# A hybrid attention and state-space block on one core: dense pieces in 26 of 28 attention steps, the second merge gate among them, and GpSimd's low parts at other steps

## The chip, the cores and the metric
The kernel runs on one core of a Trainium2 chip. A time is microseconds of device time of one execution. The kernel before took 439.01, 440.55 and 440.67 us in three runs, median 440.55.

TensorE multiplies (its plain name in the rows is PE, its weight loads PEld), VectorE is DVE, ScalarE is ACT, GpSimd is POOL, and SyncE (SP) issues nearly all DMAs. SBUF is the working memory, PSUM the eight accumulation banks of 128 x 512 float32 that TensorE writes.

## What is computed
One block for 512 tokens of width 1024, in float32:

```python
h = rmsnorm(x, norm_g)
(q, kc, vc, ksl, vsl, kwi, vwi, gl, gate_nsa, u, gate_s5, mg) = split(h @ w_in)
# NSA: 8 heads in 2 groups; three branches, each softmax(q k) v
#   compressed keys (compress(kc), compress(vc)), selected blocks (ksl, vsl, rotary), window (kwi, vwi, rotary)
o_nsa = sum over branches of sigmoid(gl) * branch
branch_a = (o_nsa * silu(gate_nsa)) @ w_proj_nsa
# S5: 32 groups of 16 channels, 64 complex states, diagonal recurrence over the tokens
y = Re(C scan(A, B u)) + D u;  z = gelu(y)
o_s5 = z * sigmoid(z @ w_glu + b_glu)
branch_b = (o_s5 * silu(gate_s5)) @ w_proj_s5
merged = sigmoid(mg_a) * branch_a + sigmoid(mg_b) * branch_b
out = rmsnorm(x + merged @ w_out, final_g)
```

## The kernel before
**Precision by three products.** Each large matmul is done as three of the faster float32r type: both factors are split into a high part and a low part (the rest), and TensorE adds high x low, low x high and high x high (`mm3`, L1043 to L1045). ScalarE makes the high part of each weight block (`split_hi`, L768), GpSimd the low part (L723, `lo_done`), from raw blocks that SyncE loads three ahead in a fixed order (`weight_blocks`). A block's split buffers are two, so its high part waits until the block two ahead of it is used. A dense job is one 128 x 512 output in a bank, over 8 K tiles (4 for the `glu` jobs) of three matmuls each.

**Order by hand.** There is no scheduler: each engine's program is written out, and `bank_plan` numbers the fills and reads of each PSUM bank, so that `open_bank`, `wait_fill` and `wait_drained` are waits on two semaphores for each bank.

**The S5 part.** States are computed in chunks of 4 tokens. Inside a chunk the output needs the products KR (lag by lag) shifted down by 48, 32, 16 and 0 rows within each half of the partitions: the table TT. Before, TensorE does the shift with a matrix of ones (`shift`, a constant that is loaded) and the identity, into banks TT0 and TT1 (L1181), between the jobs kc and vc, and ScalarE copies the two banks out. TT is used first by the Y matmuls (L1289), just ahead of attention. Y goes through memory to be reordered (`y_through_scratch`, 16 stores of L552, then one load of yT). VectorE adds D u to yT (L1850), ScalarE makes the GELU of it (L988), which needs a table load before it and one behind it, and VectorE and GpSimd split z for the GLU.

**Attention.** 24 steps, six for each of four head pairs (two branches, three sets of query tiles: tile 3 alone, tiles 0 and 1, tile 2), and four more turns for what trails. In step s each engine does, in this order:
- TensorE: scores of s (L1320), transposes of the probabilities of w = s - 3 (L1338), a dense piece if `FILL` has one for s, and the weighted values of w - 1 (L1359). Where a new job starts right behind another piece, the values go ahead of the piece. The values of a head pair add up in bank 6; the first of a pair (L1351, from peT) waits until VectorE has taken the last pair out.
- VectorE: the copy of the transposed probabilities of w out of bank 4 (L1813; for some w that of bank 5 too, else ScalarE does it), in steps 10, 16 and 22 `gate_pair` (L1788, and L1790 the high part), the product of a dense job that ended in step s - 1 (`fill_part`, L1778, and for a glu job L1770, L1470 and L1776), the masking with its row minimum (L1804), and `normalise` of s - 1 (L1827).
- ScalarE: copies of bank 5, the exponentials of s (L975), and the tanh of a job that ended in s (L942).
- GpSimd: low parts, each held back by `behind_normalise(s)` until VectorE has normalised step s, which is at the end of VectorE's step s + 1.

`FILL` names the first and last step of each dense job. All go to bank 7 but those in `FILL_BANK`. `D_TERM_AT`, `GELU_AT` and `Z_SPLIT_AT` say in which steps the sum with D, the GELU and the high part of z are done. Behind the loop, the merge gates MA and MB and the projections A and B follow for eight column blocks (the B jobs need all of f, the A jobs the low part of the last head pair), then the output projection, the residual and the last norm, whose four row tiles are stored in halves (L643, L645).

Before, gn1 runs in steps 0 to 5, gn2 in 6 to 9, glu0 in 12 and 13, glu1 in 15 and 16, gn3 in 18 to 20, glu2 in 22 and 23, glu3 in 24 and 25 (bank 0), MB0 in 26 and 27 (bank 1), and MB1 behind the loop.

Of the kernel before, what the change touches and what calls it, by code (L numbers as in the profile page):

```python
# [19 lines left out]
F32 = mybir.dt.float32  # L20
# [5 lines left out]
P = 128  # L26
# [47 lines left out]
O_LOW_AHEAD = ["gn3", "glu1"]  # L74
F_LOW_AFTER = ["gn3", "glu1", "mgb0", "mgb1"]
O_LOW_AFTER = ["mgb0", "pb0"]


# [20 lines left out]
def tile_offsets(tiles):  # L99
# [22 lines left out]
D_TERM_AT, GELU_AT, Z_SPLIT_AT = (4, 5), (6,), (7, 8)  # L122
BOTH_COPIES = (3, 4, 5)
# [3 lines left out]
LOW_BEHIND = dict(gn3=10, glu1=16, mgb0=20)  # L127
O_LOW_BEHIND = (9, 15, 21)
F_LOW_BEHIND = (13, 17, 23)


def bank_plan():
# [42 lines left out]
    use("TT0", 0)  # L175
    use("TT1", 1)
# [49 lines left out]
def build_program(nc, a, out):  # L226
# [16 lines left out]
    with ctx:  # L243
# [3 lines left out]
        def shared(name, size, *sets):  # L247

            made = {}
            for tensors in sets:  # L250
                with ExitStack() as once:
# [50 lines left out]
                   [("TT", [P, GP, CH, SC], F32), ("below_u", [P, 1024], F32), ("U_sh", [P, GP, NCH], F32)],  # L302
# [3 lines left out]
        TT, U_sh, yT, f_hi, f_lo = (m[n] for n in ("TT", "U_sh", "yT", "f_hi", "f_lo"))  # L306
# [5 lines left out]
        m = shared("room_5", 640, [("KR", [P, GP, SC], F32), ("shift", [P, CH - 1, P], F32)],  # L312
                   [("hidn", [GROUPS * NC, 2, 256], F32)], [("k_hi_0", [P, T], F32R)])
        KR, shift, hidn, k_hi_0 = (m[n] for n in ("KR", "shift", "hidn", "k_hi_0"))
# [91 lines left out]
        khi_done, qhi_done, k_split, q_split = (sem(n) for n in ("k_hi_done", "q_hi_done", "k_split", "q_split"))  # L406
        starts_set, pool_carry = sem("run_starts_set"), sem("gpsimd_carry")
# [116 lines left out]
        def _(sp):  # L524
# [41 lines left out]

            def load(dst, src, s):
                sp.dma_start(dst, src).then_inc(s, 16)
# [27 lines left out]
            for k, (name, split) in enumerate(blocks):  # L596
# [4 lines left out]
                if k == NRAW + 2:  # L601
                    const_loads()
# [47 lines left out]
        def _(pl):  # L650
            pl.wait_ge(dt_row_in, 16)
            nc.gpsimd.tensor_copy(par_rows[0:GP, 2, :].rearrange("p (r n) -> p r n", r=2),
                                  dt_in[0:GP, :].unsqueeze(2).broadcast_to((GP, 2, SN))).then_inc(dt_spread, 1)
            nc.gpsimd.memset(flat_k[:, :, :, NC - 1:NC], 0.0).then_inc(flat_zero, 1)
            nc.gpsimd.memset(kcT[:, :, :], 0.0).then_inc(kc_zero, 1)
            nc.gpsimd.memset(flat_v[:, :, :, NC - 1:NC], 0.0).then_inc(flat_zero, 1)
# [17 lines left out]
            def query_low(n, s=None):  # L674

                pl.wait_ge(qhi_done, n + 1)
                if s is not None:
                    behind_normalise(s)
                nc.gpsimd.tensor_tensor(qr_lo[:, n, :], qr[:, n, :], q_hi[n].bitcast(F32),
                                        ALU.subtract).then_inc(q_split, 1)  # L680

# [20 lines left out]
            for j, name in enumerate(split_names):  # L702
# [6 lines left out]
                if name == "gn3":  # L709
                    query_low(2, 8)  # L710
                if name in O_LOW_AHEAD:
                    c = O_LOW_AHEAD.index(name)
                    pl.wait_ge(ohi_done, c + 1)
                    behind_normalise(O_LOW_BEHIND[c])
                    nc.gpsimd.tensor_tensor(oT_lo[:, c, :], tmp[:, 1, :], oT_hi[:, c, :].bitcast(F32),
                                            ALU.subtract).then_inc(oT_split, 1)
# [1249 lines left out]
```

## Time and profile before
| what | value |
|---|---|
| timed runs | 439.01, 440.55, 440.67 us |
| the profiled execution | 440.01 us, its span 438.2 us |
| TensorE busy | 420.4 us, 96% |
| VectorE / ScalarE / GpSimd busy | 281.6 / 200.9 / 169.4 us |
| mean granted clock of TensorE | 0.988 of full speed |
| attention, first scores to the end of MB1 | 152.63 to 266.96 us |

A row of the timeline has start, duration, engine, line, operation, output <- inputs and how often, and in brackets how long the engine was idle before it and for whom. The granted clock is 1.00 at 2.4 GHz and 0.50 at 1.2 GHz.

### The profile page before, as it was taken

What the parts mean: (1) busy time and instruction counts of PE and PEld (TensorE: products, weight loads), DVE (VectorE), ACT (ScalarE), POOL (GpSimd) and SP (SyncE); (2) the same over time, 40 slices, a digit from 0 to 9 for tenths busy, and PEclk for the clock granted to TensorE, in tenths of its full rate; (3) what the DMA queues carried; (4) which work ended last, traced back from release to release, by engine and by line L of the source; (5) the groups of instructions that cost most, each with busy time, mean ns of one, the idle gap of its engine ahead of it and who ended that gap; (6) DMA issues with size and microseconds to landing.
All of it is one profiled execution on the core that took longest, in us unless ns stands there. A gap on an engine that the chain in (4) does not pass through costs nothing.

```text
span 438.2 us, 7325 instructions
## 1 busy us (share of the span) xinstructions
PE 420.4 (96%) x2776; PEld 342.4 (78%) x2776; DVE 281.6 (64%) x641; ACT 200.9 (46%) x394; POOL 169.4 (39%) x92
## 2 busy tenths in 40 slices
PE   5899999999999997899999999999999999999994
PEld 5788888898778875667677778888888888888994
DVE  3779996999999997699998952071071071170544
ACT  6644759714235675857467432222222222231433
POOL 0444323333369402154141344454454454454430
PEclk9999999999999999799999999999999999999998
DMA  8998993224841254101001113933333333333105
GB/s 286 153 276 209 177 250 111 60 71 120 249 96 49 51 99 144 48 2 49 1 6 46 49 49 101 328 79 113 100 81 111 97 88 101 101 96 97 48 1 191
DMA packets 71458, 48.05 MB, mean 110 GB/s; under 512 B 20272, under 2 KB 66816, under 8 KB 71424
## 3 DMA queue, kind: packets, MB, share of 16 engines
q1 hardware_dynamic: 71264, 47.53, 41.8%
q8 instruction: 22, 0.36, 0.4%
q14 instruction: 12, 0.10, 0.1%
q10 hardware_dynamic: 160, 0.07, 0.1%
HBM read 43.39 MB, written 4.19 MB: 109 GB/s over the span
## 4 chain that ended last, share of the span: by engine, by line
PE 86%; DVE 5%; DMA 3%; issue 2%; SPq 2%; ACT 1%; POOL 1%; POOLq 1%; DVEq 0%; ACTq 0%
PE bank L1043 23%; PE bank L1045 22%; PE bank L1044 22%; PE bank L1359 3%; PE bank L1338 3%; PE bank L1320 2%; PE bank L1211 2%; SPq L552 2%; DMA yT<-y_scratch 1%; DVE prob L1804 1%; PE bank L1088 1%; DVE prob L1827 1%; PE bank L1157 1%; DMA hid<-in_norm_g 1%; DVE probT L1813 1%
## 5 line engine op out<-in xcount | busy, mean ns | idle before, releaser
L723 POOL TENSOR_TENSOR w_lo<-raw,w_hi 128x1024 fp32r<-128x1024 f32 (+3 forms) x56 | 133.8, 2388 | 181.2 <-ACT w_hi L768 166.8
L1043 PE MATMUL bank<-hT_lo,w_hi 128*128 128x512 f32 x288 | 115.7, 402 | 4.6 <-DVE tmp L1778 3.4
L1045 PE MATMUL bank<-hT_hi,w_hi 128*128 128x512 f32 x288 | 112.8, 392 | 0.0
L1044 PE MATMUL bank<-hT_hi,w_lo 128*128 128x512 f32 x288 | 112.7, 391 | 0.0
L768 ACT ACTIVATE w_hi<-raw 128x1024 fp32r<-128x1024 f32 (+2 forms) x56 | 58.4, 1043 | 73.9 <-PE bank L1045 73.3
L1043 PEld LDWEIGHTS bank<-hT_lo,w_hi 128*128 128x128 f32 x288 | 54.3, 189 | 18.0 <-issue 7.2
L1045 PEld LDWEIGHTS bank<-hT_hi,w_hi 128*128 128x128 f32 x288 | 54.3, 189 | 11.6
L1044 PEld LDWEIGHTS bank<-hT_hi,w_lo 128*128 128x128 f32 x288 | 54.4, 189 | 10.5
L975 ACT ACTIVATE prob<-prob,nmax 128x128 f32<-128x128 f32 (+2 forms) x64 | 35.3, 553 | 27.1 <-DVE nmax L1804 27.1
L1004 ACT ACTIVATE tmp<-bank 128x512 f32<-128x512 f32 x16 | 9.5, 597 | 59.6 <-PE bank L1045 57.2
L1869 DVE SCALAR_TENSOR_TENSOR tmp<-tmp,bank 128x512 f32<-128x512 f32 x8 | 5.5, 688 | 44.6 <-ACT tmp L1004 44.6
L1864 DVE SCALAR_TENSOR_TENSOR tmp<-tmp,bank 128x512 f32<-128x512 f32 x8 | 5.5, 687 | 40.1 <-ACT tmp L1004 32.7
L1804 DVE CUSTOM_DVE_ANT_0 prob<-bank,causal 128x128 f32<-128x128 f32 (+2 forms) x64 | 27.9, 483 | 0.0
L1827 DVE TENSOR_SCALAR prob<-prob,coef,gate 128x128 f32<-128x128 f32 (+2 forms) x64 | 26.1, 460 | 0.9
L1043 PE MATMUL bank<-w_lo,m_hi 128*128 128x256 f32 (+1 forms) x80 | 26.1, 326 | 0.3 <-POOL f_lo L723 0.3
L1044 PE MATMUL bank<-w_hi,m_lo 128*128 128x256 f32 (+1 forms) x80 | 26.0, 325 | 0.0
L1045 PE MATMUL bank<-w_hi,m_hi 128*128 128x256 f32 (+1 forms) x80 | 26.0, 325 | 0.0
L1338 PE MATMUL bank<-ident,prob 128*128 128x128 f32 x160 | 23.1, 284 | 0.3 <-DVE probT L1813 0.3
L1359 PEld LDWEIGHTS bank<-probT,v_tok 128*64 128x64 f32 x288 | 16.1, 136 | 9.3 <-issue 7.4
L1464 DVE TENSOR_TENSOR bank<-X,bank 128x512 f32<-128x512 f32 (+4 forms) x42 | 22.2, 528 | 1.5
L1359 PE MATMUL bank<-probT,v_tok 128*64 128x128 f32 (+1 forms) x288 | 22.5, 291 | 0.0
L1338 PEld LDWEIGHTS bank<-ident,prob 128*128 128x128 f32 x160 | 17.6, 143 | 6.1 <-issue 4.1
(255 smaller groups left out, 768.5 us busy)
## 6 DMA issues: line engine op xcount, KB each, us to landing
raw<-in_w_in SPq DMA_DIRECT2D x28, 512.0 KB, 3.8
raw<-in_w_in SPq DMA_DIRECT2D x16, 256.0 KB, 4.0
raw<-in_w_out SPq DMA_DIRECT2D x8, 512.0 KB, 3.7
x_sb<-in_x SPq DMA_DIRECT2D x4, 512.0 KB, 5.1
raw<-in_w_proj_s SPq DMA_DIRECT2D x4, 512.0 KB, 3.4
raw<-in_w_proj_nsa SPq DMA_DIRECT2D x8, 256.0 KB, 3.9
r_sb<-in_x SPq DMA_DIRECT2D x1, 2048.0 KB, 8.5
out<-r_sb SPq DMA_DIRECT2D x8, 256.0 KB, 2.2
```

The source lines that it names most:

```text
L723: nc.gpsimd.tensor_tensor(lo, whole, hi.bitcast(F32), ALU.subtract).then_inc(lo_done, 1)
L768: nc.scalar.activation(split_views(name)[0], view(raw, k % NRAW, dims), ACT.Copy)\
L975: nc.scalar.activation(pi, pi, ACT.Exp, scale=-1.0, bias=nmax[:, s % 4, g, k:k + 1], accum_out=den[:, s % 4, g, k:k + 1]).then_inc(e_done, 1)
L1004: drain(nc.scalar.activation(tmp[:, 0, :], bk(f"{kind}{d}")[:, :], ACT.Tanh, scale=0.5), f"{kind}{d}")
L1043: nc.tensor.matmul(dst, w[0], x[1], start=first, stop=False, skip_group_check=True)
L1044: nc.tensor.matmul(dst, w[1], x[0], start=False, stop=False, skip_group_check=True)
L1045: return nc.tensor.matmul(dst, w[0], x[0], start=False, stop=last, skip_group_check=True)
L1338: ins = nc.tensor.transpose(bk(job)[:, col:col + P], prob[:, w % 4, g, c + P * kt:c + P * kt + P], ident[:, :])
L1359: ins = nc.tensor.matmul(o[DH * g:DH * g + DH, P * at[0][0]:P * at[0][0] + n], v_tok[:, kt, b, DH * g:DH * g + DH], probT[:, 2 * (w % 2) + ...
L1464: link(V.tensor_tensor(o, x, y, op))
L1804: drain(V.tensor_tensor_reduce(prob[:, s % 4, g, c:c + n], bk(job)[:, c:c + n], causal[:, T - n:T], 1.0, 3.0e38, ADD, ALU.min, nmax[:, s % ...
L1827: V.tensor_scalar(pi, pi, coef[:, s % 4, g, k:k + 1], gate[:, i, HPG * g + r, 1 + b:2 + b], MUL, MUL)\
```

## The change
The table TT is no longer made on TensorE. GpSimd zeroes a buffer `lags` (behind the low part of u2), SyncE copies KR into it with seven DMAs at the four row offsets (`shifted_lags`, behind the load of kwi), and ScalarE copies `lags` into TT. The constant `shift` is gone, `rope` has a semaphore of its own, and the other four constant loads come later, ahead of kc's load. GpSimd's first small jobs go behind its first low part. The last row tile's first half is stored from ScalarE's queue.

In attention the dense jobs go to other steps: all but 5 and 10 have a piece, MB1 moves into the loop, and only MB1 has another bank than 7. The D term, the GELU and the z split come one step later, as do the steps in which VectorE copies both banks. `gate_pair` goes ahead of the copy and its high part behind it, and GpSimd's low parts of the weights, of oT and of f stand at other steps.

```diff
-FILL = dict(gn1=(0, 5), gn2=(6, 9), glu0=(12, 13), glu1=(15, 16), gn3=(18, 20), glu2=(22, 23), glu3=(24, 25),
-            MB0=(26, 27))
-FILL_BANK = dict(glu3=0, MB0=1)
+FILL = dict(gn1=(0, 4), gn2=(6, 9), glu0=(11, 12), glu1=(13, 14), gn3=(15, 17), glu2=(18, 19), glu3=(20, 21),
+            MB0=(22, 24), MB1=(25, 27))
+FILL_BANK = dict(MB1=1)
...
-D_TERM_AT, GELU_AT, Z_SPLIT_AT = (4, 5), (6,), (7, 8)
-BOTH_COPIES = (3, 4, 5)
+D_TERM_AT, GELU_AT, Z_SPLIT_AT = (5, 6), (7,), (8, 9)
+BOTH_COPIES = (4, 5, 6)
...
-LOW_BEHIND = dict(gn3=10, glu1=16, mgb0=20)
-O_LOW_BEHIND = (9, 15, 21)
-F_LOW_BEHIND = (13, 17, 23)
+LOW_BEHIND = dict(gn3=11, glu1=14, mgb0=18, mgb1=21)
...
+            def shifted_lags():
+
+                wait_drained(sp, "KR")
+                sp.wait_ge(lags_zero, 1)
+                for j in range(CH):
+                    down = SC * (CH - 1 - j)
+                    for first, last in ((0, SN), (SN, P)) if down else ((0, P),):
+                        sp.dma_start(lags[first + down:last, j], KR[first:last - down]).then_inc(lags_in, 16)
...
             def const_loads():
-                load(shift[:, :, :], a["shift"], consts_in)
-                load(rope[:, :, :], a["rope"], consts_in)
...
                 if k == NRAW + 2:
+                    load(rope[:, :, :], a["rope"], rope_in)
+                if k == NRAW + 7:
                     const_loads()
...
+                if name == "kwi":
+                    shifted_lags()
...
             for i in range(NT):
-                sp.wait_ge(y_ready[i], 1)
-                sp.dma_start(out[0, P * i:P * i + P, 0:512], r_sb[:, i, 0:512]).then_inc(stored, 16)
+                if i < NT - 1:
+                    sp.wait_ge(y_ready[i], 1)
+                    sp.dma_start(out[0, P * i:P * i + P, 0:512], r_sb[:, i, 0:512]).then_inc(stored, 16)
...
+                elif name == "gn3":
+                    oT_low(0, 10)
+                    query_low(3, 12)
+                    f_low(0, 13)
+                elif name == "glu1":
+                    f_low(1, 15)
+                    oT_low(1, 16)
+                elif name == "mgb0":
+                    f_low(2, 20)
+                elif name == "mgb1":
+                    f_low(3, 22)
+                    oT_low(2, 22)
+                elif name == "pb0":
+                    oT_low(3)
...
-            pe.wait_ge(consts_in, 16 * 4)
-
-            wait_drained(pe, "KR")
-            for k in range(2):
-                open_bank(pe, f"TT{k}")
...
+                pair_ends = s >= 10 and s % 6 == 4
+                if pair_ends:
+                    gate_pair((s - 10) // 6)
                 if 0 <= w < NS:
                     copy_probs(w)
-                if s >= 10 and s % 6 == 4:
-                    gate_pair((s - 10) // 6)
+                if pair_ends:
+                    pair_high((s - 10) // 6)
```

The order of instructions at two places. The first is VectorE at the start of step 10, with the last rows of step 9. Before:

```order
L1823 RECIPROCAL coef<-den 128x2 [waits exp_done]
L1827 TENSOR_SCALAR prob<-prob,coef,gate 128x384 [waits dve_chain]
L1827 TENSOR_SCALAR prob<-prob,coef,gate 128x384
L1813 COPY probT<-bank4 128x384 [waits pv_done,bank4_filled]
L1788 TENSOR_TENSOR tmp<-bank6,tmp 128x512 [waits bank4_drained,pv_done]
L1790 CAST oT_hi<-tmp 128x512 [waits bank6_drained]
L1778 SCALAR_TENSOR_TENSOR sg_third<-tmp,bank7 128x512 [waits tanh_done]
```

And after:

```order
L1834 RECIPROCAL coef<-den 128x2 [waits exp_done]
L1838 TENSOR_SCALAR prob<-prob,coef,gate 128x384 [waits dve_chain]
L1838 TENSOR_SCALAR prob<-prob,coef,gate 128x384
L1870 CAST z_hi<-z 128x512 [waits z_done] x2
L1796 TENSOR_TENSOR tmp<-bank6,tmp 128x512 [waits bank4_drained,pv_done]
L1824 COPY probT<-bank4 128x384 [waits pv_done,bank4_filled]
L1801 CAST oT_hi<-tmp 128x512 [waits bank6_drained]
L1786 SCALAR_TENSOR_TENSOR sg_third<-tmp,bank7 128x512 [waits tanh_done]
```

The gate of the pair (tmp<-bank6) has moved ahead of the copy, and the second pair of z_hi casts now stands between the normalise of step 8 and the gate.

The second place is GpSimd from the low part of the third query on (qr_lo is a query's, oT_lo a head pair's, f_lo the GLU output's, w_lo a weight block's: gn3, glu1, mgb0 in this order). Before:

```order
L679 TENSOR_TENSOR qr_lo<-qr,q_hi_mid 128x512
L715 TENSOR_TENSOR oT_lo<-tmp,oT_hi 128x512
L723 TENSOR_TENSOR w_lo<-raw,w_hi 128x1024
L679 TENSOR_TENSOR qr_lo<-qr,q_hi_ends 128x512
L665 TENSOR_TENSOR f_lo<-z,f_hi 128x512
L715 TENSOR_TENSOR oT_lo<-tmp,oT_hi 128x512
L723 TENSOR_TENSOR w_lo<-raw,w_hi 128x1024
L665 TENSOR_TENSOR f_lo<-z,f_hi 128x512
L723 TENSOR_TENSOR w_lo<-raw,w_hi 128x1024
```

And after:

```order
L686 TENSOR_TENSOR qr_lo<-qr,q_hi_mid 128x512
L737 TENSOR_TENSOR w_lo<-raw,w_hi 128x1024
L694 TENSOR_TENSOR oT_lo<-tmp,oT_hi 128x512
L686 TENSOR_TENSOR qr_lo<-qr,q_hi_ends 128x512
L672 TENSOR_TENSOR f_lo<-z,f_hi 128x512
L737 TENSOR_TENSOR w_lo<-raw,w_hi 128x1024
L672 TENSOR_TENSOR f_lo<-z,f_hi 128x512
L694 TENSOR_TENSOR oT_lo<-tmp,oT_hi 128x512
L737 TENSOR_TENSOR w_lo<-raw,w_hi 128x1024
```

The weight parts have moved ahead of the low parts of the first and second head pair.

## Rows read from the trace of the kernel before
**Rows 1.** Page, section 2: TensorE's granted clock in 40 slices of 10.95 us.
```profile
PEclk9999999999999999799999999999999999999998
```
**Rows 2.** Waits of TensorE: who waited for whom, us in total, times, longest.
```profile
PE bank L1043 <- DVE tmp L1778: 3.4, 1, 3.4
PE bank L1351 <- DVE tmp L1788: 1.5, 3, 0.9
```
**Rows 3.** Timeline of TensorE around the shift of KR: start us, us, what.
```profile
85.44 0.39 PE L1043 MATMUL bank<-hT_lo,w_hi 128*128 128x512 f32 x1
...
86.13 1.46 PE L1181 MATMUL bank<-KR,shift 128*128 128x256 f32 x6
...
88.55 0.39 PE L1043 MATMUL bank<-hT_lo,w_hi 128*128 128x512 f32 x1
```
**Rows 4.** Timeline of TensorE, steps 5 to 10.
```profile
167.15 0.88 PE L1338 MATMUL bank<-ident,prob 128*128 128x128 f32 x6
...
176.38 0.77 PE L1043 MATMUL bank<-hT_lo,w_hi 128*128 128x512 f32 x1 [3.44 <-DVE tmp L1778]
...
193.22 0.88 PE L1338 MATMUL bank<-ident,prob 128*128 128x128 f32 x6
195.01 1.08 PE L1351 MATMUL bank<-peT,v_blk 128*64 128x512 f32 x4 [0.92 <-DVE tmp L1788]
```
**Rows 5.** Windows: length, busy us of each engine, granted clock, DMA share, GB/s.
```profile
174.50:175.00 0.50, 0.00 (x0) 0.00 (x0) 0.50 (x2) 0.00 (x0) 0.50 (x1) 0.97 0.00 0
...
181.50:182.00 0.50, 0.50 (x5) 0.50 (x5) 0.27 (x1) 0.50 (x2) 0.00 (x0) 0.70 0.00 0
```
**Rows 6.** Timeline of VectorE, step 4: the sum of y with D.
```profile
168.91 1.41 DVE L1850 SCALAR_TENSOR_TENSOR yT<-u_perm,pcol,yT 128x512 f32<-128x512 f32 x2 [2.19 <-DMA yT<-y_scratch]
```
**Rows 7.** Windows of steps 5, 6 and 7 to 9 of VectorE, the third engine.
```profile
170.24:178.40 8.16, 4.71 (x31) 3.54 (x32) 8.09 (x23) 4.25 (x10) 2.54 (x1) 0.79 0.07 11
181.73:193.15 11.42, 11.42 (x95) 8.41 (x93) 11.15 (x36) 8.92 (x22) 5.08 (x4) 1.00 0.01 1
```
**Rows 8.** Timeline of ScalarE around the GELU of z.
```profile
178.42 1.28 ACT L988 ACT_TABLE_LOAD   x1
...
179.72 3.90 ACT L988 ACTIVATE z<-yT 128x512 f32<-128x512 f32 x4
183.63 1.28 ACT L975 ACT_TABLE_LOAD   x1
```
**Rows 9.** Timeline of step 13 on three engines.
```profile
204.22 0.87 PE L1338 MATMUL bank<-ident,prob 128*128 128x128 f32 x6
...
206.40 1.09 PE L1359 MATMUL bank<-probT,v_tok 128*64 128x128 f32 x16
...
204.88 0.54 DVE L1813 COPY probT<-bank 128x384 f32<-128x384 f32 x1
205.34 0.28 DVE L1804 CUSTOM_DVE_ANT_0 prob<-bank,causal 128x128 f32<-128x128 f32 x1
...
207.28 0.49 ACT L975 ACTIVATE prob<-prob,nmax 128x256 f32<-128x256 f32 x1
```
**Rows 10.** Timeline of GpSimd and VectorE: products of z with and without a low part.
```profile
254.22 2.38 POOL L723 TENSOR_TENSOR w_lo<-raw,w_hi 128x1024 fp32r<-128x1024 f32 x1 [1.46 <-ACT w_hi L768]
...
254.49 2.67 DVE L1770 SCALAR_TENSOR_TENSOR z<-tmp,z 128x512 f32<-128x512 f32 x1
...
209.20 0.68 DVE L1770 SCALAR_TENSOR_TENSOR z<-tmp,z 128x512 f32<-128x512 f32 x1
```
**Rows 11.** Timeline of SyncE (loads of kwi and kc) and ScalarE (KR, kc).
```profile
52.13 3.70 SPq L628 DMA_DIRECT2D raw<-in_w_in  x2
...
61.97 0.41 ACT L778 ACTIVATE KR<-bank 128x256 f32<-128x256 f32 x1
...
74.38 1.04 ACT L768 ACTIVATE w_hi<-raw 128x1024 fp32r<-128x1024 f32 x1
```
**Rows 12.** Timeline of SyncE's queue: the last two stores.
```profile
435.11 0.33 SPq L643 DMA_DIRECT2D out<-r_sb  x1
435.49 0.43 SPq L645 DMA_DIRECT2D out<-r_sb  x1
```

More of the change, by code:

```diff
@@ L680, in query_low, with oT_low, f_low @@
                                         ALU.subtract).then_inc(q_split, 1)
+            def oT_low(c, s=None):
+                pl.wait_ge(ohi_done, c + 1)
+                if s is not None:
+                    behind_normalise(s)
+                nc.gpsimd.tensor_tensor(oT_lo[:, c, :], tmp[:, 1, :], oT_hi[:, c, :].bitcast(F32),
+                                        ALU.subtract).then_inc(oT_split, 1)
+            def f_low(t, s):
+                behind_normalise(s)
+                low_part(f_lo, z, f_hi, (t,), fhi_done, f_split)
             def carry_last_groups():
@@ L879, in _ @@
             after("kc")
+            ac.wait_ge(lags_in, 16 * (2 * CH - 1))
             for k in range(2):
-                evacuate(f"TT{k}", TT[:, :, 2 * k:2 * k + 2, :].rearrange("p g j c -> p j g c"),
-                         bk(f"TT{k}")[:, :].rearrange("p (j g c) -> p j g c", j=2, c=SC))
+                lag = slice(2 * k, 2 * k + 2)
+                nc.scalar.activation(TT[:, :, lag, :].rearrange("p g j c -> p j g c"), lags[:, lag], ACT.Copy).then_inc(tt_built, 1)
             after("vc")
@@ L990, in _ @@
                                              ACT.Gelu_apprx_tanh).then_inc(z_done, 1)
-                if s in pieces and s == FILL[pieces[s][0]][1] and pieces[s][0] != "MB0":
+                if s in pieces and s == FILL[pieces[s][0]][1] and pieces[s][0] not in ("MB0", "MB1"):
                     fill_part(pieces[s][0])
+                if s == FILL["MB0"][1]:
+                    after("mgb0")
             for dp in range(4):
@@ L1000, in _ @@
                         wait_fill(ac, f"{kind}{d}")
-                        if gate_first:
-                            after(f"mgb{d}")
+                        if gate_first and d == 1:
+                            after("mgb1")
                         tanh_free(f"{user}{d}")
@@ L1172, in _ @@
             channel_major("kc", "kc")
-            pe.wait_ge(consts_in, 16 * 4)
-            wait_drained(pe, "KR")
-            for k in range(2):
-                open_bank(pe, f"TT{k}")
-                for jj in range(2):
-                    j = 2 * k + jj
-                    down = shift[:, j, :] if j < CH - 1 else ident[:, :]
-                    ins = nc.tensor.matmul(bk(f"TT{k}")[:, 256 * jj:256 * jj + 256], down,
-                                           KR[:, :, :].rearrange("p g c -> p (g c)"), start=True, stop=True,
-                                           skip_group_check=True)
-                fill(ins, f"TT{k}")
             channel_major("vc", "vc")
@@ L1724, in _ @@
             wait_fill(ve, "H")
+            ve.wait_ge(consts_in, 16 * 2)
             for m in range(2):
@@ L1831, in _ @@
                 w = s - LAG
+                pair_ends = s >= 10 and s % 6 == 4
+                if pair_ends:
+                    gate_pair((s - 10) // 6)
                 if 0 <= w < NS:
                     copy_probs(w)
[L1834 to L1836 removed]
+                if pair_ends:
+                    pair_high((s - 10) // 6)
+                if s - 1 in pieces and s - 1 == FILL[pieces[s - 1][0]][1] and pieces[s - 1][0] not in ("MB0", "MB1"):
                     fill_part(fills, pieces[s - 1][0])
```

75 lines of the change are left out of this document (27 added, 48 removed).

## Prediction
> **What bounds the kernel now.** I read three views in this order. The busy slices of the page: TensorE's clock row stands at 9 in nearly every slice, with one 7 at 175 to 186 us [rows 1]. The waits of TensorE: the longest inside the kernel is 3.4 us, for the product that takes gn1's gate out of bank 7 (L1778); three waits of 1.5 us together are for the gate of a finished head pair (L1788) [rows 2]. The timelines around the long wait: TensorE had nothing from 172.94 to 176.38 [rows 4], the granted clock left full speed at 174.98 and came back at about 181.7 [rows 5], so 5.3 us of resumed work ran at 1.2 instead of 2.4 GHz, which lost 2.65 us. So the kernel is bound by TensorE's stream of matmuls; a change gains what it takes from that stream, from its waits, and from the clock that a wait costs. In attention VectorE is close behind: between 170.24 and 193.15 it is idle for no more than 0.35 but in the 3.3 us between 178.40 and 181.73, in which TensorE crawled [rows 7]. A time below is in microseconds of the span of before; the profiled execution took 440.01 (span 438.2 and 1.8 around it), the three timed runs 439.01, 440.55 and 440.67.
>
> **Part 1, the lag table TT by DMA.** TensorE drops 8 matmul records that ran from 86.13 on. vc's second K tile started at 88.55; without them it starts one tile of 0.68 (three matmuls) behind 86.13, at 86.81: 1.74 gained [rows 3]. VectorE's chain up to attention is not fed by it, but its last link, the products of the compressed branch, waits for ScalarE and GpSimd work that does move; I take it as moving along, with 0 to 0.75 lost if one of its products falls under a GpSimd low part. On SyncE seven DMAs for the lags and four constant loads now stand between kwi's load (52.13, [rows 11]) and kc's, and the first waits until KR is out at 62.38 [rows 11]. Eleven issues at 0.33 to 0.43 [rows 12] put kc's load at about 67, landing some 4 later, 3 before ScalarE wants it at 74.38 [rows 11]. That cover hides all of it; vc's load goes with it and is wanted only 7.6 later. The zeroing of the lags and the later small GpSimd work sit in waits. The ScalarE copies stay two.
>
> **Part 2, steps 0 to 10.** The Y round trip through memory made VectorE wait 2.19 at step 4 [rows 6]. Now its sum with D stands in steps 5 and 6, behind more work, and y, which moves 1.74 with TensorE, is there first. That ends the old stall: gn1 is done at step 4, its product is in step 5, and gn2 starts at step 6. What is late next? I walk it. TensorE's transposes of step 5 began at 167.15 [rows 4]; they come 1.74 earlier for part 1 and 1.36 later, since all 8 K tiles of gn1 instead of 6 are ahead of them: 166.8. VectorE's copy follows the start of transposes by 0.66 [rows 9]: 167.4. Its steps 5 to 9 took 19.4 in before (8.16 and 11.42 less a short wait, [rows 7]); now all four sums with D lie in them instead of two (1.33 more, half of [rows 6] being 0.7 each), less 0.1 to 0.4 of blocked time: 20.6. And ScalarE delays it. Its GELU, now behind the exponentials of step 7, takes 1.28 + 3.90 + 1.28 with its table loads [rows 8]. The masking of step 7 starts at 177.5, its exponentials end 2.43 later [rows 9], the GELU and loads end at 186.4, the two exponentials of step 8 at 187.7; VectorE wants them at 186.4 and loses 1.3. Its step 10 begins at 189.3, and the head-pair gate, now first in it, is done at 190.0. TensorE is at that point long before: its transposes of step 10 began at 193.22, 26.07 behind those of step 5 [rows 4]; without stall, slow clock and two K tiles this is 18.6, so 185.4, done at 186.1. So it waits 3.9, at a step that has no dense piece: **the stall moves from step 6 to step 10 and does not shrink**. The values of pair 1 start at 190.0 instead of 195.01: 5.0 ahead. But 3.9 of idling is longer than the 3.44 after which the clock had fallen, so I charge the same 2.65 behind it. The unknown here is 0 to 3.9 for the wait (at 0 if VectorE ran 4 us faster), and 0 or 2.65 for the clock.
>
> On the table loads the Trainium skill ("ScalarE: Activation LUTs", section "What ACT_TABLE_LOAD costs") says that a switch costs a drain of some 1.38 us beside the 1.28 of the load. The trace shows none: the GELU ends at 183.62, the load starts at 183.63 and [rows 8] leave no room for a drain. By that rule the gate would come 2.8 later and the time would be 442.8; the sum goes by the rows.
>
> **Part 3, steps 11 to 27.** Work is the same: 40 K tiles before the first B block on either side. Gone are the other two gate waits, 0.6 [rows 2], since gate_pair now stands ahead of the copy. New is that glu1, gn3, glu2, glu3 and MB0 each start in bank 7 one step after the piece ahead of them ended there, so each waits for a VectorE product. At step 13 TensorE is ready 1.65 behind the start of transposes (0.63 of transposes and 1.02 of values, [rows 9] with the step's end at 207.42); VectorE needs 0.66 + 0.47 + 0.69 [rows 9, 10], so 0.2. But GpSimd's weight parts, 2.38 long, now start with steps 13 and 20, just ahead of the products of glu0 and glu2, and a product with both inputs in SBUF stands until GpSimd ends: 254.49 took 2.67 and ended 0.56 behind the end of the low part, against 0.68 alone [rows 10]. From the walk: step 13 loses 0.7, step 15 1.2 (VectorE is late by then, with f_low under its product), 18 0.25, 20 0.95, 22 0.2: 3.3, of which the range is 1.0 (no collision, five times 0.2) to 5. The skill ("SBUF — State Buffer", "Who interferes with whom") calls this an exclusive lock that goes to the one that issued first; by it and by the rows the loss is the same.
> MB1 inside the loop fills slots but adds no time. Behind the loop the last pair's low part has only B0 and B1 (5.5) to hide under, and needs 2.7, then pa0's low part 2.4: 0.4 is left, so nothing is charged; if one is late, A0 waits 0.5.
>
> **Part 4, the end.** The last two stores now leave from two queues: the second no longer stands behind 0.33 of issue and its gap, 435.49 to 435.11 [rows 12]: 0.35 gained.
>
> **Sum.** 5.0 gained up to pair 1, 2.65 given to the clock, 0.6 gained, 3.3 given to bank 7, 0.35 gained: 0.0. So 440.0 against the profiled execution; the median of the runs is 0.5 above that, and I say 440.3.
>
> **The rivals.** (a) The clock holds, or the wait of step 10 is short enough for it: 2.65 less, 437.6. For it speaks that the clock fell only 2 us into the old idle time, so a wait under 2 would be harmless; against it that my walk has 3.9. (b) VectorE keeps up: wait of step 10 under 1, collisions mild. Then 3.9, 2.65 and about 1.5 of the 3.3 come back: 432.3. For it: its steps hold gaps I may have over-counted; against: they are counted from rows. (c) Slower: the late VectorE of steps 13 to 15 meets f_low(0) and the glu1 part so that gn3's wait in step 15 reaches 3.5 instead of 1.2; from there the clock falls again. 2.3 + 2.65 on top: 445.2. It decides once that wait passes about 2 us. (d) The kc load comes too late, for more bytes are ahead of it: it would have to be over 5 late (3 of cover and 2.7 between GpSimd's part and TensorE's need), and each further one counts in full: 442 or more.
>
> **How the numbers follow.** Forecast 0.58 (own range 438.2 to 442.4, from 1.0 to 5 for bank 7 and 0.75 for the compressed branch), (a) 0.18, (b) 0.10, (c) 0.10, (d) 0.04. The range is 435.5 to 443.5: below it lies most of (b), 0.08, above it some 0.10 of (c) and (d), and it takes in (a) with the bank-7 term at its low end. A measurement here tells 0.5% (2.2 us) from no change. Faster by more, under 438.3: (b), most of (a) and an edge of the forecast, 0.30; slower by more: (c), (d) and an edge, 0.16; within: 0.54.
>
> **What would show it.** The waits of TensorE in the new profile: none at step 6, one of 3 to 4.5 on the peT matmul of pair 1, with a low clock behind it; 0.5 to 1.5 each at the starts of glu1, gn3 and glu3, put down to L1770's product. ScalarE's GELU at 181 to 185 and VectorE idle about 1 us ahead of the normalise of step 8. No row for shift, 1.7 earlier gs0. If TensorE has no wait over 2 us at step 10, the walk of part 2 is wrong, and (a) or (b) holds.

## The result, and the profile after

The changed kernel took **443.18 us** in the median of 6 runs (442.72 to 444.06) against 439.78 for the kernel before (6 runs, 438.66 to 441.11). The ratio on record is 1.0062, 95% interval 1.0039 to 1.0084; the two medians by themselves stand 0.8% apart. It is slower by 0.6%, small but outside its interval, where I had forecast no change (440.3, range 435.5 to 443.5). Its profiled execution took 442.79, with a span of 441.0 against 438.2.

The clock row of the page (section 2, 40 slices, now of 11.0 us) answers to [rows 1]; the waits of TensorE answer to [rows 2] (us in total, times, longest):

```profile
PEclk9999999999999999989999999999999999999999
```

```profile
PE bank L1360 <- DVE tmp L1796: 4.1, 1, 4.1
PE bank L1065 <- DVE z L1778: 2.7, 3, 1.0
PE bank L1065 <- DVE CT L1601: 1.8, 1, 1.8
...
PE bank L1298 <- ACT Y_sb L796: 1.1, 1, 1.1
```

The 3.4 at gn1's gate is gone, and 4.1 on the peT matmul of pair 1 has come, as forecast. So have the starts of glu1, gn3 and glu3 in bank 7 (2.7). But two waits stand there that I had not foreseen: one for CT, one for Y_sb. TensorE's timeline has them all (start us, us, what, wait in brackets); the rows from 187.96 on answer to [rows 4]:

```profile
41.40 0.47 PE L1065 MATMUL bank<-hT_lo,w_hi 128*128 128x512 f32 x1 [1.76 <-DVE CT L1601]
...
150.85 0.45 PE L1298 MATMUL bank<-U_sh,TT 64*64 64x128 f32 x8 [1.07 <-ACT Y_sb L796]
...
187.96 0.88 PE L1347 MATMUL bank<-ident,prob 128*128 128x128 f32 x6
192.97 1.36 PE L1360 MATMUL bank<-peT,v_blk 128*64 128x512 f32 x4 [4.14 <-DVE tmp L1796]
...
207.80 0.47 PE L1065 MATMUL bank<-z_lo,w_hi 128*128 128x512 f32 x1 [0.72 <-DVE z L1778]
...
216.88 0.47 PE L1065 MATMUL bank<-hT_lo,w_hi 128*128 128x512 f32 x1 [1.02 <-DVE z L1778]
...
231.52 0.47 PE L1065 MATMUL bank<-z_lo,w_hi 128*128 128x512 f32 x1 [0.23 <-DVE tmp L1786]
...
240.53 0.47 PE L1065 MATMUL bank<-z_lo,w_hi 128*128 128x512 f32 x1 [0.94 <-DVE z L1778]
```

**The wait at 41.40.** q0 opens the bank that VectorE still reads as CT. VectorE's setup is a chain of some 40 tiny instructions. Here it is in the changed kernel, on VectorE and then on GpSimd (pieces of the two timelines):

```profile
26.27 0.85 DVE L1474 TENSOR_SCALAR s5p<-s5p 128x16 f32<-128x16 f32 x1
...
29.56 2.36 DVE L1471 TENSOR_TENSOR s5p<-s5p,pcol 128x16 f32<-128x16 f32 x1
...
35.09 2.27 DVE L1567 COPY powers<-s5p 128x16 f32<-128x16 f32 x1
...
39.79 0.68 DVE L1598 TENSOR_SCALAR CS<-bank 64x512 f32<-64x512 f32 x1
```

```profile
26.14 0.96 POOL L766 MEMSET lags<- 128x1024 f32 x1
29.50 2.39 POOL L737 TENSOR_TENSOR w_lo<-raw,w_hi 128x1024 fp32r<-128x1024 f32 x1 [2.40 <-ACT w_hi L786]
34.94 2.40 POOL L737 TENSOR_TENSOR w_lo<-raw,w_hi 128x1024 fp32r<-128x1024 f32 x1 [3.05 <-ACT w_hi L786]
```

The zeroing of the lags holds one tiny instruction (0.85 instead of 0.17). By those 0.7 us the chain slides under the low part of u3 (a product of 0.2 takes 2.36) and, 2.7 late by then (35.09 instead of 32.42), under that of q0 (a copy of 0.17 takes 2.27). In the kernel before, the same chain's last product pair began at 29.49 and was through; the low part began at 29.71, and CS was written at 35.00:

```profile
29.49 0.38 DVE L1464 TENSOR_TENSOR s5p<-s5p 128x16 f32<-128x16 f32 x2
...
35.00 0.68 DVE L1591 TENSOR_SCALAR CS<-bank 64x512 f32<-64x512 f32 x1
```

So VectorE comes to CS 4.8 late and TensorE waits 1.76. The Trainium skill ("SBUF — State Buffer", "Who interferes with whom") says that with both inputs in SBUF a product contends with a GpSimd instruction that reads SBUF, and that a copy or a tensor_scalar can contend too; all three kinds stand in these rows, and the trace agrees.

**The wait at 150.85.** ScalarE empties the Y banks behind the exponentials of the compressed branch, and these came late:

```profile
144.69 1.50 DVE L1745 TENSOR_TENSOR e_cmp<-e_cmp,nmax_c 128x512 f32<-128x512 f32 x1
...
146.29 1.28 ACT L941 ACT_TABLE_LOAD   x1 [3.14 <-DVE e_cmp L1745]
...
150.06 1.20 ACT L796 ACTIVATE Y_sb<-bank 128x256 f32<-128x256 f32 x4
```

**Milestones.** The first scores (attention's start) came at 153.63 instead of 152.63; the values of pair 1 at 192.97 instead of 195.01; the first matmul of B0 at 269.71 instead of 267.10; the last matmul at 434.76 instead of 432.00. From the first scores to pair 1 the change gained 3.0, and I had forecast 3.3. The forecast was lost ahead of attention: 1.0 late where I had 1.74 early, which is 2.74 of the 2.8 by which the profiled execution missed it. Behind pair 1 it went a little better than forecast: 4.8 lost up to the last matmul, where I had 5.35.

### The profile page after: what moved, and what is told of

Its sections match the earlier page's. It is cut to its first block, busy times and chain, and to the rows that moved or that the text cites. A ratio compares the mean times of both kernels' runs of the same rounds, so it can differ in the third digit from the quotient of the medians.

```text
span 441.0 us, 7320 instructions
## 1 busy us (share of the span) xinstructions
PE 418.3 (95%) x2768; PEld 338.8 (77%) x2768; DVE 283.1 (64%) x641; ACT 201.2 (46%) x394; POOL 170.8 (39%) x93
## 4 chain that ended last, share of the span: by engine, by line
PE 62%; DVE 23%; ACT 5%; issue 3%; SPq 3%; DMA 2%; POOL 1%; POOLq 1%; DVEq 0%; ACTq 0%
PE bank L1065 17%; PE bank L1067 16%; PE bank L1066 16%; DVE bank L1471 5%; DVE X L1471 5%; PE bank L1329 3%; PE bank L1347 3%; PE bank L1368 3%; DMA raw<-in_w_in 2%; DVE s5p L1471 1%; DVE prob L1815 1%; PE bank L1360 1%; DVE z L1778 1%; ACT w_hi L786 1%; ACT z L1006 1%
## 5 line engine op out<-in xcount | busy, mean ns | idle before, releaser
L1824 DVE COPY probT<-bank 128x384 f32<-128x384 f32 (+1 forms) x24 | 14.4, 599 | 14.1 <-PE bank L1347 14.0
L1368 PE MATMUL bank<-probT,v_tok 128*64 128x128 f32 (+1 forms) x288 | 23.4, 300 | 0.0
```

Source lines behind the costliest of these rows:

```text
L1368: ins = nc.tensor.matmul(o[DH * g:DH * g + DH, P * at[0][0]:P * at[0][0] + n], v_tok[:, kt, b, DH * g:DH * g + DH], probT[:, 2 * (w % 2) + ...
L1824: drain(V.tensor_copy(probT[:, 2 * (w % 2), 0:n], bk(f"PT0_{w}")[:, 0:n]), f"PT0_{w}")
```

## Experiments: where the start is lost

Ten more kernels and a second profile each of the two kernels follow. They ran in three batches, each with its own runs of the kernel before, whose median was 440.17 (e1 to e4), 440.24 (e5 to e8) and 441.05 (e9 to e12); so kernels of different batches are compared by their ratios. In the tables "scores" is the start of the first scores, "to B0" the time from there to the first matmul of B0, "waits" the sum of TensorE's waits in that stretch, and "clock" what it lost by a low clock: busy time times (1 - granted clock), over windows of half a us from 170 to 202.

**e1_zero_later: the zeroing at another place.**

```diff
-                if name == "u2":
+                if name == "q1":
                     nc.gpsimd.memset(lags[:, :, :, :], 0.0).then_inc(lags_zero, 1)
```

> The changed kernel with one instruction moved: GpSimd zeroes the lags behind the low part of q1 instead of behind that of u2. My theory (A): in the profile of the changed kernel the zeroing ran at 26.14 for 0.96 us and held one of VectorE's many tiny instructions (0.85 instead of 0.17); by that 0.7 us the chain behind it slid under two GpSimd low parts (a 0.2 us product took 2.36, a 0.17 us copy 2.27), came 4.8 us late, made TensorE wait 1.76 at the start of q0 (41.40) and, through a late e_cmp, ScalarE drain a Y bank late (1.07 at 150.85). Behind q1 VectorE works out of PSUM, so both waits go: 2.8 less than the changed kernel, about 440.3, and TensorE reaches the first scores at 150.8 instead of 153.6. Rival (B): the two waits come from something else in part 1 (the GpSimd work that now stands behind its first low part, or the order of the loads); then nothing changes, 443.2.

Measured: 442.53 (12 runs), ratio 1.0046, interval 1.0021 to 1.0070. Both theories miss: the wait for CT only shrank to 1.11, and the one for Y_sb stayed (1.05). The timeline says why. Without any zeroing in its way the chain was still caught by the low parts of u3 and q0:

```profile
29.44 2.53 DVE L1471 TENSOR_TENSOR s5p<-s5p 128x16 f32<-128x16 f32 x2
...
34.93 2.51 DVE L1471 TENSOR_TENSOR pwt<-powers 128x32 f32<-128x32 f32 x2
...
40.80 0.47 PE L1065 MATMUL bank<-hT_lo,w_hi 128*128 128x512 f32 x1 [1.11 <-DVE CT L1601]
```

So of the 1.76 in the changed kernel the zeroing itself makes 0.65; the other 1.11 is a slide that comes without it.

**e2_zero_in_before: the zeroing added to the kernel before.**

```diff
+                if name == "u2":
+                    nc.gpsimd.memset(below_u[:, :], 0.0)
```

> The kernel before with one instruction added: GpSimd zeroes 128x1024 elements that nothing reads, behind the low part of u2, where the changed kernel zeroes its lags. Theory (A), the knife edge of the small VectorE chain: the same slide as in the changed kernel, TensorE waits about 1.8 at q0 and up to 1.1 at Y: 1.8 to 2.8 slower than before, 441.6 to 442.6. Theory (B), the zeroing sits in a wait and costs nothing: as before, 439.8.

Measured: 441.11, ratio 1.0015, interval 0.9992 to 1.0039. The wait at q0 is made as in the changed kernel (the tiny instruction takes 0.86, CS comes at 39.91, TensorE waits 1.76), and the first scores are 2.1 late; there is no wait for Y_sb. The time shows only 0.9 of it, and its interval reaches zero. It is also the first sign that the runs of before have part of this loss in them already.

**e3_lags_alone: part 1 without the rest** (the zeroing behind q1's low part; attention and the end as before).

```diff
-                    ins = nc.tensor.matmul(bk(f"TT{k}")[:, 256 * jj:256 * jj + 256], down,
-                                           KR[:, :, :].rearrange("p g c -> p (g c)"), start=True, stop=True,
...
+                    for first, last in ((0, SN), (SN, P)) if down else ((0, P),):
+                        sp.dma_start(lags[first + down:last, j], KR[first:last - down]).then_inc(lags_in, 16)
```

> The kernel before with part 1 alone (TT from shifted copies of KR by DMA, its loads in their new places), the zeroing behind q1's low part, attention and the end as before. By my sum: 1.74 us of TensorE work gone, the loads hidden, so 438.1 (ratio 0.996); the step-6 stall stays, since the Y round trip moves along with TensorE. Rival: the loads that stand 16 us later than before (kc at 71.0 instead of 55.4) or a product of the compressed branch under a low part take some of it back: 438.5 to 439.8.

Measured: 439.56, ratio 0.9986, interval 0.9958 to 1.0014. A slide again (CS at 39.34, 1.12 at q0), and the wait for Y_sb is there too (1.06): it belongs to part 1, not to the slide.

**e4_attention_alone: the changed kernel without part 1**, so TT comes from the shift matmuls and nothing is zeroed.

> The changed kernel without part 1: TT comes from the shift matmuls again, nothing is zeroed, attention, the low parts and the end as changed. The traces give 285.57 us from the first scores to the end in the kernel before and 287.37 in the changed one, so attention and the end cost 1.8 by themselves: 441.6 (ratio 1.004). By my prediction's walk they cost 1.7. Rival: the late VectorE of the first part of the changed kernel is what made its attention slow (step 10's wait of 4.14), and with an early start this is 1 to 3 faster than that: 438.6 to 440.6.

Measured: 443.60, ratio 1.0066, interval 1.0039 to 1.0093, where a ratio of 1.004 was expected, which is just inside the interval. It also slid (CS at 39.35, 1.12 at q0), and it had no wait for Y_sb. The stretch to B0 took 116.77, a little more than in the changed kernel. Since the slide made its first scores late as well (153.96), it says nothing on the rival of an early start; e6_after_gated below does.

So three kernels (e1_zero_later, e3_lags_alone, e4_attention_alone) slid though GpSimd had nothing new ahead of u3's low part but small things of 0.3 us, or nothing at all (e3_lags_alone). The question became whether the kernel before slides as well. Two experiments answer it.

**e11_before_again: the kernel before, a second profile.**

> The kernel before, unchanged, for a second profile. Theory (C): it stands on the edge, so another execution may well show VectorE's tiny product under u3's low part (2.2 us instead of 0.2), VectorE at CS at 39 instead of 35.0 and a wait of TensorE for CT of about 1.1 at q0. Theory (D): it never slides; CS at 35.0 and no such wait.

It took 439.97 (one run) and it slid:

```profile
29.48 2.52 DVE L1464 TENSOR_TENSOR s5p<-s5p 128x16 f32<-128x16 f32 x2
...
40.83 0.47 PE L1043 MATMUL bank<-hT_lo,w_hi 128*128 128x512 f32 x1 [1.10 <-DVE CT L1594]
```

with the low part at 29.58. Of two profiles of the kernel before one slides and one doesn't; the second product of the pair starts some 0.2 behind its first, so at 29.70 against a low part at 29.71 in the one, at 29.69 against 29.58 in the other. In the three kernels above, too, the low part was first (29.55 against 29.65, 29.70 against 29.77, 29.70 against 29.84). **The profile on which I predicted was the lucky one at this place.** Over the whole kernel it was not: it took 440.01 and the one that slid 439.97. The slide brought the first scores 1.15 later, and by pair 1 all of it was made up (195.01 and 194.95), for the wait of step 6 was 0.35 shorter and the low clock happened to cost 1.0 less.

**e5_before_gated, e6_after_gated, e7_lags_gated: the slide made impossible.** GpSimd waits with two low parts until VectorE has left the chains that they could hold. Both low parts still end ahead of TensorE's need. In e6_after_gated and e7_lags_gated the zeroing also stands behind q1's low part.

```diff
+                if name == "u3":
+                    wait_copied(pl, "B")
+                if name == "q0":
+                    wait_copied(pl, "CT0")
```

> The kernel before with two waits added on GpSimd: the low part of u3 starts only when VectorE has begun to read the B bank (its first chain of tiny products is behind it), the low part of q0 only when it has read CT0 (its powers are done). The first batch showed that the slide of VectorE's setup under these two low parts (2.2 + 2.3 us) happens without any zeroing too, in a run of the changed kernel without part 1 and in two with the zeroing later; the shown profile of the kernel before escaped it by some 0.02 us (a product at 29.70, the low part at 29.71). Theory (C), the kernel before stands on that edge by itself and its runs are a mix of both cases: with the waits it never slides, no wait of TensorE at q0, VectorE reads CT0 at 35.0, and the median is 0.5 to 1.5 below that of before. Theory (D), the kernel before never slides and only changed programs do: same as before, or slower by what the low parts lose.

> The changed kernel with the zeroing behind q1's low part and the same two waits on GpSimd. Theory: the wait at q0 (1.76) and the one at Y (1.07) both go, TensorE reaches the first scores at 150.9 instead of 153.6, attention costs what it did (+2 against the kernel before), so 440.3 +- 0.5. Rival: attention is paced by VectorE from step 5 on whatever comes before, and the 2.8 come back as a longer wait at step 10: 442 to 443.

> The kernel before with part 1 alone and the two waits on GpSimd. Theory: no wait at q0 or Y, so part 1 is worth what I said of it, 1.74 us of TensorE against the gated kernel before; 437.5 to 438.3. Rival: the wait of step 6 for gn1's gate, which Y's round trip paces, grows by what the start gains: 439 or more.

| kernel | median | ratio (95%) | CS at | at q0 | for Y_sb | scores |
|---|---|---|---|---|---|---|
| before, first profile | 439.78 | | 35.00 | 0 | 0 | 152.63 |
| before, e11_before_again | 439.97 | | 39.22 | 1.10 | 0 | 153.78 |
| changed | 443.18 | 1.0062 (1.0039-1.0084) | 39.79 | 1.76 | 1.07 | 153.63 |
| e5_before_gated | 439.64 | 0.9993 (0.9975-1.0012) | 35.74 | 0 | 0 | 152.78 |
| e7_lags_gated | 438.43 | 0.9957 (0.9941-0.9974) | 35.72 | 0 | 1.05 | 152.07 |
| e6_after_gated | 441.43 | 1.0024 (1.0013-1.0035) | 35.51 | 0 | 1.05 | 151.77 |

The two waits on GpSimd end the slide in all three; what is left of it is one copy that takes 0.49 instead of 0.17. What follows:
- The slide costs the changed kernel some 0.38% or 1.7 us (1.0062 to 1.0024; by the two intervals 0.1% to 0.6%; first scores 153.63 to 151.77). The kernel before gains 0.07% by them, within its interval; I had expected 0.5 to 1.5 us. That its runs are a mix is shown by its two profiles; how often each case comes, and so why the waits win it so little, is not.
- The wait for Y_sb stays in all with part 1. In the gated kernels the exponentials of the compressed branch start at 143.37 without part 1 and at 144.42 in e6_after_gated; TensorE comes to the Y banks 1.75 earlier (first of them at 145.39 in e7_lags_gated, at 147.14 in e5_before_gated). VectorE's product there takes 1.50 with part 1 (142.82, under a low part that now starts earlier, at 141.37 instead of 143.43) and 0.69 without (142.38). So 0.8 of the 1.05 by which the exponentials come later is this collision; without it, by these rows, a wait of some 0.2 would be left (an estimate, not run).
- So part 1 brings the first scores 0.7 forward, from 152.78 to 152.07, and not 1.74. In time it is worth 1.2 us (439.64 to 438.43): **part 1 alone, gated, beats the kernel before** by 0.43% (0.26% to 0.59%).
- e6_after_gated was to be at 440.3 and is at 441.43; against e7_lags_gated attention and the end cost 3.0. It starts attention earliest of all with the new one, and its stretch to B0 is 116.86: an early start doesn't help.

## Experiments: attention

Eleven profiles have the old attention or the new one under different starts. The stretch to B0, taken apart:

| kernel | attention | to B0 | waits | clock | rest |
|---|---|---|---|---|---|
| before | old | 114.47 | 5.26 | 2.71 | 106.50 |
| e11_before_again | old | 113.25 | 5.11 | 1.71 | 106.43 |
| e3_lags_alone | old | 112.85 | 6.26 | 0 | 106.59 |
| e5_before_gated | old | 113.18 | 5.01 | 1.65 | 106.52 |
| e2_zero_in_before | old | 114.65 | 6.51 | 1.69 | 106.45 |
| e7_lags_gated | old | 114.88 | 5.49 | 3.05 | 106.34 |
| changed | new | 116.08 | 7.05 | 1.71 | 107.32 |
| e12_after_again | new | 116.00 | 7.02 | 1.57 | 107.41 |
| e4_attention_alone | new | 116.77 | 7.04 | 2.54 | 107.19 |
| e6_after_gated | new | 116.86 | 7.04 | 2.64 | 107.18 |
| e1_zero_later | new | 116.75 | 7.05 | 2.43 | 107.27 |

In the mean the new attention takes 2.6 more (116.5 against 113.9): 1.4 of it in waits, 0.4 by the clock, 0.8 in the rest.

**e12_after_again: the changed kernel, a second profile.**

> The changed kernel, unchanged, for a second profile. The slide is to be there in any execution (the zeroing alone shifts the chain by 0.7, far more than its spread of 0.1): a wait of 1.76 for CT at q0, one of about 1.05 for Y_sb, 4.1 at step 10. Open is the low clock behind step 10: 3.35 us of it in the first profile, 1.7 us lost; the profiles of the gated and the later-zeroing kernels show more.

It took 442.98 (one run), with 1.76 for CT, 1.05 for Y_sb and 4.13 at step 10.

The rest, TensorE's own work, is the same within 0.25 in each group, and **0.8 more in the new attention**. The dense work up to B0 is 56 K tiles on either side, but the new one is cut into more pieces, and a piece costs its edges. In the kernel before MB1 runs in one piece, from 261.51 to the first matmul of B0 at 267.10: 5.59 for 8 tiles. In the changed kernel it is three pieces, of 2, 3 and 3 tiles:

```profile
261.50 0.50 PE L1065 MATMUL bank<-hT_lo,w_hi 128*128 128x512 f32 x1
...
262.99 0.82 PE L1347 MATMUL bank<-ident,prob 128*128 128x128 f32 x6
263.57 0.47 PE L1065 MATMUL bank<-hT_lo,w_hi 128*128 128x512 f32 x1
...
265.81 0.87 PE L1368 MATMUL bank<-probT,v_tok 128*64 128x256 f32 x8
266.61 0.50 PE L1065 MATMUL bank<-hT_lo,w_hi 128*128 128x512 f32 x1
...
268.90 0.88 PE L1368 MATMUL bank<-probT,v_tok 128*64 128x128 f32 x12
```

1.49, 2.24 and 2.29, together 6.02, so 0.2 for each further cut. That accounts for about half of the 0.8 (26 pieces instead of 24); where the other half is, I have not located.

**e8_no_gelu_table: what of step 10's wait is ScalarE's.** S5's GELU is computed as tanh, so S5's output has other values; no table is loaded for it.

```diff
-                                             ACT.Gelu_apprx_tanh).then_inc(z_done, 1)
+                                             ACT.Tanh).then_inc(z_done, 1)
```

> The gated changed kernel (zeroing later, two waits) with one function changed: S5's GELU in attention step 7 is computed as tanh, which needs no table load; so 2.56 us of loads leave ScalarE between the exponentials of steps 7 and 8 and the output's values are others. It measures how much of the wait of step 10 (4.14) is ScalarE's: by my walk VectorE lost 1.3 there (1.65 in the trace). Theory: VectorE's idle 1.65 at 188.9 goes, the wait of step 10 becomes 2.5 and the time falls by 1.6 against the gated changed kernel, by more if the clock then holds (1.7 on top). Rival: VectorE is late by its own work and the wait stays near 4.

Measured: 437.45 (6 runs), ratio 0.9946, interval 0.9925 to 0.9966; 4.0 below the gated changed kernel.

```profile
189.23 1.08 PE L1364 MATMUL bank<-peT,v_blk 128*64 128x512 f32 x4 [2.21 <-DVE tmp L1800]
```

The wait fell by 1.9, a little more than the 1.6 expected, and the clock held (no loss, against 2.64). So of the 4.14, 1.9 is made by the two table loads, and the fall of the clock mostly hangs on it: the mean granted clock is 0.997 or 0.998 in four of the six runs and 0.993 or 0.994 in the other two, which took 1.6 more, against 0.990 to 0.994 in all twelve of e6_after_gated. With the clock, 1.9 of wait cost 4 in the median.

**e9_gate_early and e10_gate_z_early: VectorE's order.** In the changed kernel VectorE stands still for 1.65 in step 9, while the gate product that TensorE waits for could run (the values of pair 0 are complete):

```profile
188.84 0.08 DVE L1815 DVE_READ_ACCUMULATOR2_ANT nmax<- 128x1 f32 x1
190.57 0.17 DVE L1834 RECIPROCAL coef<-den 128x2 f32<-128x2 f32 x1 [1.65 <-ACT prob L993]
190.77 0.87 DVE L1838 TENSOR_SCALAR prob<-prob,coef,gate 128x384 f32<-128x384 f32 x2
191.56 0.76 DVE L1870 CAST z_hi<-z 128x512 fp32r<-128x512 f32 x2
192.23 0.69 DVE L1796 TENSOR_TENSOR tmp<-bank,tmp 128x512 f32<-128x512 f32 x1
```

```diff
                     for g in range(GROUPS):
                         masked(s, g)
+                if s == 9:
+                    gate_pair(0)
                 if 1 <= s <= NS:
                     normalise(s - 1)
```

The second kernel has the casts of z's tiles 2 and 3 there as well:

```diff
                 if s == 9:
                     gate_pair(0)
+                    for t in tiles_at(s, Z_SPLIT_AT):
+                        ve.wait_ge(z_done, t + 1)
+                        V.tensor_copy(z_hi[:, t, :], z[:, t, :]).then_inc(zhi_done, 1)
```

> The gated changed kernel with VectorE's gate product of pair 0 moved from the start of step 10 into step 9, between the masking and the normalise that waits 1.65 us for ScalarE's exponentials; the values of pair 0 are complete there (TensorE's last of them run at 186.3 in the changed kernel). It tests what the wait of step 10 is: if VectorE's order makes it (my theory), TensorE goes on at 189.7 instead of 193.0, the wait shrinks from 4.14 to about 0.9, the clock holds (1.7 to 2.4 more), and the next limit is GpSimd's low part of z, which glu0 needs and which ends at 195.1: a wait of about 2 for z_split at step 11. Together 3 to 4 below the gated changed kernel, 437.4 to 438.4. Rival: VectorE is late by its work, and the copies of steps 10 and 11 (probT) bring the wait back one step later: within 1 of 441.4.

> As the one with the early gate product, and the second half of z's high parts (0.76 us) moved to the same place in step 9, ahead of the normalise. Gate and high parts are 1.45 together and fit into the 1.65 in which VectorE waits; GpSimd's second low part of z then ends at about 193 instead of 195.1, when TensorE comes to glu0. Theory: no wait over 1 at steps 10 and 11, 5 to 5.7 below the gated changed kernel: 435.7 to 436.4. Rival: the high parts wait for the last GELU tile (187.9) and the table load behind it, GpSimd's low part stands in the way of the normalise (both work on SBUF alone), and it is no better than the gate product alone.

Measured: 439.50, ratio 0.9964 (0.9944 to 0.9984), and 439.12, ratio 0.9957 (0.9935 to 0.9978). The kernel before was at 441.05 on that chip, so ratios are to be compared: 0.60% and 0.67% below the gated changed kernel, 2.6 and 3.0 us, of an expected 3 to 4 and 5 to 5.7; the second falls short by half. The wait of step 10 is gone to 0.76, and the next ones appear, first in the one, then in the other kernel:

```profile
187.63 1.08 PE L1364 MATMUL bank<-peT,v_blk 128*64 128x512 f32 x4 [0.76 <-DVE tmp L1800]
...
190.98 0.52 PE L1351 MATMUL bank<-ident,prob 128*128 128x128 f32 x3 [0.67 <-DVE probT L1828]
...
192.47 0.52 PE L1351 MATMUL bank<-ident,prob 128*128 128x128 f32 x3 [0.98 <-ACT probT L800]
```

```profile
191.74 0.52 PE L1351 MATMUL bank<-ident,prob 128*128 128x128 f32 x3 [1.47 <-DVE probT L1828]
...
196.44 0.50 PE L1333 MATMUL bank<-k_hi,qr_lo 64*128 64x512 f32 x2 [1.27 <-POOL qr_lo L686]
```

In e10_gate_z_early the rival's mechanism is in the timeline of VectorE: the normalise of step 8 now meets GpSimd's low part of z and takes 2.32 instead of 0.87.

```profile
188.81 2.32 DVE L1842 TENSOR_SCALAR prob<-prob,coef,gate 128x384 f32<-128x384 f32 x2
```

So the order of VectorE made the wait of step 10, but VectorE was also late by its work: about half of what the early gate gives TensorE comes back within two steps. Both kernels, with part 1 and the gating in them, beat the kernel before by as much as e7_lags_gated does with the old attention.

## Why the prediction was wrong

Its working, part by part, against the profiles.

- **Part 1, the step that failed.** "VectorE's chain up to attention is not fed by it, but ... I take it as moving along, with 0 to 0.75 lost", and nothing in the sum. The chain did not move along. In e6_after_gated the first product behind it starts at 141.31, in e5_before_gated, without part 1, at 140.88, while TensorE came 1.75 earlier. And a GpSimd low part that did move held one of its products for 0.8: that collision I had named, at the right size, and put at nothing. TensorE lost 1.05 of the 1.74 (e7_lags_gated).
- **Part 1, a second failed step.** "The zeroing of the lags and the later small GpSimd work sit in waits", costed at nothing. The zeroing does sit in a wait of GpSimd, but not of VectorE, which had tiny SBUF instructions there. The slide cost 1.76 at q0, and some 1.7 in time. The zeroing makes it certain and 0.65 longer, and 1.1 comes without it in four other profiles, one of the kernel before among them; the profile that I had read was one without. I had weighed this collision for products in attention [rows 10], where it lengthens one product, and not for a chain of 40 instructions, where 0.7 of delay was turned into 4.8 by the next two low parts. Nor had I seen that the kernel before stood 0.01 us from the same slide.
- The kc load at 71.0 instead of 67 hid all the same; rival (d) did not come.
- **Part 2, right.** The old stall gone, a wait of 4.14 at step 10 (3.9 forecast), at the instruction that I named. The gain up to pair 1, from the first scores, was 3.0 (3.3). That it came so near is in part luck: against the second profile of the kernel before, which lost less by the clock, it is 1.8. The charge for the clock, 2.65, is the top of what such a wait cost in five profiles (1.57 to 2.64), and in this one it cost 1.71. The argument of rival (a), that a wait under 2 would be harmless, does not hold: in e9_gate_early none was over 0.98 and the clock fell.
- **Part 3.** The bank-7 waits are 0.72, 1.02, 0.23 and 0.94, 2.9 together, against 0.7, 1.2, 0.25, 0.95 and 0.2: right. The other gate waits gave 0.9 instead of 0.6 (one for probT went too). Wrong was "MB1 inside the loop fills slots but adds no time": the new attention has 0.8 more of TensorE's own time.
- **Part 4, wrong.** 0.35 was to be gained. From the end of the last matmul to the end of the span it is 5.9 in both. The store of the low half now leaves from ScalarE's queue at 437.87, while the other leaves from SyncE's at the same time, and both together end no sooner than the two did one behind the other [rows 12]. The last issue is 0.35 earlier behind the last matmul (2.85 instead of 3.20), as forecast, but it takes 2.69 instead of 2.31 to land:

```profile
435.37 2.86 SPq L650 DMA_DIRECT2D out<-r_sb  x2
...
437.87 0.40 ACTq L1058 DMA_DIRECT2D out<-r_sb  x1
```

**The sum again**, in the profiled execution: 1.76 (slide), 1.07 (Y_sb), 0.8 (pieces), 0.35 (end) and 0.24 (step 10) more than I had; 0.95 (clock), 0.4 (bank 7) and 0.3 (gates) less: 2.6 on top of my 0.0. Measured are 2.8. Nearly all of it lies in terms that I had set to nothing; of the terms that I worked out, each came within 0.5 but the clock's. That behind the first scores the errors cancel, 1.4 too little against 1.65 too much, is luck. The time was inside the range only because rivals (c) and (d) had stretched it, by other mechanisms: gn3's wait was 1.02, not 3.5.

Two things are not in the sum. From B0 to the last matmul the changed kernel took 0.15 more. And the 442.8 that stands beside the table loads starts from 440.0, while the rivals start from 440.3; on their base it is 443.1, all but the measured time. That is a coincidence: the changed kernel has no drain at its table loads either (load at 182.64, GELU from 183.94 to 187.93, load at 187.94, exponentials from 189.23).

## What to carry to other kernels

When work leaves the bounding engine, ask of each chain beside it whether it is fed by what left; one that isn't keeps its time and becomes the next wait. Here each GpSimd low part that started in a chain of tiny VectorE instructions with operands in SBUF held it to that low part's end, so nothing on GpSimd "sits in a wait" until VectorE's timeline at that place has been read, and a low part that may wait a little is better gated behind the chain. And read two profiles before building on gaps of hundredths of a microsecond.

## What the runs showed of the hardware

- **The price of a wait in clock is not fixed by its length.** With a longest wait of 2.92 the clock held (e3_lags_alone); 2.96 cost 1.65 (e5_before_gated), 3.02 cost 3.05 (e7_lags_gated), 3.09 cost 1.71 (e11_before_again), 3.44 cost 2.71 (before), 3.57 cost 1.69 (e2_zero_in_before), and 4.13 to 4.16 cost 1.57 to 2.64 in five profiles. 2.21 cost nothing (e8_no_gelu_table), nor did three waits of 0.75, 1.47 and 1.27 (e10_gate_z_early), but three of 0.76, 0.67 and 0.98 within 5 us came with a loss of 1.70 (e9_gate_early). In the changed kernel the clock was still full when TensorE went on at 192.97 and fell only behind it to 0.50 (1.2 GHz), unlike in [rows 5] (windows: length, busy us of TensorE, its weight loads, VectorE, ScalarE and GpSimd, granted clock, DMA share, GB/s):

```profile
193.00:193.50 0.50, 0.50 (x4) 0.21 (x6) 0.50 (x2) 0.50 (x1) 0.50 (x1) 1.00 0.00 0
193.50:194.00 0.50, 0.50 (x4) 0.09 (x2) 0.50 (x2) 0.50 (x2) 0.50 (x2) 0.63 0.00 0
196.50:197.00 0.50, 0.50 (x6) 0.29 (x2) 0.28 (x1) 0.50 (x4) 0.05 (x1) 0.50 0.00 0
```

- **A GpSimd zeroing is enough to hold VectorE.** It only writes, and it held a 128x16 TENSOR_SCALAR for 0.7 us, in the changed kernel and in e2_zero_in_before.
- **Two stores in two queues ended no sooner than in one queue** (5.9 from the last matmul to the end in both; the last one took 2.69 to land beside the other and 2.31 behind it).
